# Expert outputs weighted on their way out of PSUM and added by the scatter to the residual rows in DRAM

## The chip, the cores and the metric

The kernel runs on one core of a Trainium2 chip. A core has TensorE (PE; its weight loads are PEld), VectorE (DVE), ScalarE (ACT), GpSimd (POOL), SyncE (SP, which issues most transfers) and 16 DMA engines between DRAM and the core's memory. The metric is the device time of one execution in microseconds (us), as the median of several runs.

## What is computed

A first block (window attention, a gated linear recurrence and a delta-rule recurrence) is followed by two layers on 16 + 1024 tokens of width 1024. Layer 0 has a short convolution as its mixer, layer 1 latent attention. Each ends in a mixture of experts with a residual, which is what the change is about:

```
h = h + mixer(rmsnorm(h, g))
h = h + hier_moe(rmsnorm(h, g2), ...)

hier_moe(x):                       # 64 experts in 8 groups, inner width 256
    grp  = argmax(x @ w_grp);  p_g = max(softmax(x @ w_grp))
    top2 = two largest of softmax(x @ w_exp) inside group grp
    gate = p_g * top_p / sum(top_p)                # two weights per token
    for each expert e:  y_e = (silu(x @ w_gate[e]) * (x @ w_up[e])) @ w_down[e]
    result[token] = sum over its two experts of gate * y_e[token]
```

After layer 0 the rows go, normed, into the latents of the attention (`w_dq`, `w_dkv`); after layer 1 a last norm gives the output, for tokens 16 to 1039.

## The kernel before, in words

Everything is fp32. `moe` runs in two blocks. `back_and_route` (not changed) makes the mixer's output rows, adds the residual and stores the sum in DRAM (`h1` in layer 0, `h3` in layer 1), stores the normed rows in `hn`, and works out for each token its two experts and its rank in each expert's list. From these it makes `queue`: for each pair of experts 128 slots, 64 per expert, row 0 with the token, row 1 with 2 x token + choice; a slot that is not used has a number out of bounds, and the transfer leaves it out. What does not fit into 64 slots of an expert goes to a "spill" loop behind the main one, which is entered only if there is such a rest.

`experts` then goes over 32 pairs of experts. The weights of a pair are 6 MB (`gate`, `up`, `down`, 2 MB each) in a ring of `RING` = 3 slots; SP issues a load as soon as the products that read the slot's old weights are done (`g_done`, `h_done`, `y_done`). For pair p:

- POOL gathers 128 rows of `hn` into `xe` two pairs ahead, as soon as PE has turned pair p (`x_turned`), and then scatters the rows of pair p-2 into `ys` (`scatter`, line 3433). `ys` has one row of 1024 for each token and each of its two choices.
- PE turns the rows (8 transposes), ACT and DVE copy them out (`rows_out`), PE makes the gate and up products (line 3249), ACT the silu, DVE `hidden`, PE turns that, ACT copies it (`hT_copy`), and PE makes the down products (line 3269) of pair p between the gate and up products of pair p+1.
- ACT and DVE copy the two halves of the result out of PSUM (`y_first`, `y_second`, called in `y_half`) into one of two buffers `ysb`; each copy waits until the scatter of two pairs ago has landed (`y_stored`).

The two gate weights per token are made by ACT (two exponentials, line 3560) and DVE (`gates`) at pair 1. The plan of the spill (`spill_plan`, DVE) stands at pair 2.

The results in `ys` are weighted and summed in the stage that follows. `combine_and_latents` (layer 0, line 3713) loads, per tile of 128 tokens, the residual rows from `h1` (0.5 MB) and the `ys` rows (1 MB) in a ring of three buffers; `make` (DVE) adds the two weighted rows with `gathered_sum` (two instructions), POOL stores the sum as `h2`, which the second layer's output stage reads again, and ACT and DVE norm the rows for PE's transposes and latent products. `combine_out` (line 4028) does the same at the end of the kernel for 8 tiles, 5 of them with sums on DVE and 3 on PE, and then norms and stores them. Residual rows of the last stage are issued behind the last weights, in `FinalLoads.start`; `ys` rows when the last scatter has landed, in `rows` (SP waits for `y_stored`). Between the blocks every engine meets in a barrier.

Of the kernel before, what the change touches and what calls it, by code (L numbers as in the profile page):

```python
# [11 lines left out]
P = 128  # L12
# [3158 lines left out]
def experts(nc, D, layer, tokens, keep, spill, gate, gu_slots, d_slots, xe, g_loaded, u_loaded, d_loaded, x_loaded, after, within):  # L3171
# [5 lines left out]
    with Phase(nc, "ex", within) as ph:  # L3177
# [18 lines left out]
        owner = ph.sb("owner", [1, SPILL_BLOCKS, EXPERTS])  # L3196
# [7 lines left out]
        sp_none = ph.sb("sp_none", [P, SPILL_PAIRS])  # L3204
        x_ps = ph.ps("x_ps", [P, 2, 512])
# [10 lines left out]
                                                       "y_stored", "w_used", "x_used", "seen"]}  # L3216
        y_stored = [ph.sem(f"y{b}_stored") for b in range(2)]
        d_ends = [ph.sem(f"d_end{k}_loaded") for k in range(2)]
        hn_dram, y_rows = D["hn"], D["ys"].rearrange("t (c d) -> (t c) d", c=2)
# [12 lines left out]
        def spill_scatter(pool, b, s, pair):  # L3232
            pool.sem_inc(s["out_ready"], 1)
            nc.gpsimd.tensor_copy(ib[:, b, 1:2], queue[:, 1, bass.ds(pair, 1)]).then_inc(s["out_ready"], 1)
            pool.wait_ge(s["out_ready"], 2)
            nc.gpsimd.indirect_dma_start(y_rows[:, :], bass.IndirectOffsetOnAxis(ap=ib[:, b, 1:2], axis=0), ysb[:, b], None,
                                         bounds_check=2 * T - 1, oob_is_err=False).then_inc(s["y_stored"], 16)
            pool.sem_clear(s["out_ready"])
# [72 lines left out]

        def spill_plan(dve, v):
# [3 lines left out]
            dve.wait_ge(id_done, 2)  # L3316
# [8 lines left out]
            v(tt(owner[:], send[0:1].unsqueeze(1).to_broadcast([1, SPILL_BLOCKS, EXPERTS]),  # L3325
                 blocks[0:1].unsqueeze(2).to_broadcast([1, SPILL_BLOCKS, EXPERTS]), ALU.is_le))
            v(red(owners[:, 0:SPILL_BLOCKS], owner[:], AX.X, ALU.add))
# [7 lines left out]
        def spill_slots(dve, v):  # L3335
# [14 lines left out]
            for n in range(2 * TT):  # L3350
                t, c, b = n // 2, n % 2, n % 2
                if n >= 2:
                    dve.wait_ge(hot_used, n - 1)
                v.hold(ts(hot_r[:, b], row[:], rest[:, t, c:c + 1], ids[:, t, c:c + 1], ALU.is_equal, ALU.mult))
                v(ts(hot_b[:, b], blocks[:], at_blk[:, t, c:c + 1], None, ALU.is_equal))
                dve.sem_inc(hot_made, 1)
            dve.wait_ge(hot_used, 2 * TT)
            found = h_ps[:, 1, 0:SPILL_PAIRS]
# [6 lines left out]
        def spill_products(pe):  # L3365

            for n in range(2 * TT):
                pe.wait_ge(hot_made, n + 1)
                for half in range(2):
                    rows = slice(CAP * half, CAP * half + CAP)  # L3370
                    last = nc.tensor.matmul(h_ps[rows, 1, 0:SPILL_PAIRS], hot_r[:, n % 2], hot_b[:, n % 2, half::2],
                                            start=(n == 0), stop=(n == 2 * TT - 1))
                last.then_inc(hot_used, 1)
# [7 lines left out]
        with nc.Block() as block:  # L3381
# [43 lines left out]
            def _(pool):  # L3425
# [30 lines left out]
                with pool.If(0 < count):  # L3456
                    pool.sem_inc(s["seen"], 1)
                    pool.wait_ge(spill_queue, 1)
                    with pool.Fori(0, SPILL_PAIRS) as i:
                        with pool.If(2 * i < count):  # L3460
# [3 lines left out]
                            spill_scatter(pool, 0, s, PAIRS_M + i)  # L3464
                            pool.wait_ge(s["y_stored"], 16 * i + 16)
# [4 lines left out]
            def _(pe):  # L3470
# [15 lines left out]
                for p in range(PAIRS_M):  # L3486
# [47 lines left out]
            def _(act):  # L3534
# [5 lines left out]
                def y_half(p):  # L3540
                    if p >= 2:
                        act.wait_ge(y_stored[p % 2], 16 * (p // 2))
                    act.wait_ge(m["y_done"], p + 1)
                    y_first(p % 2).then_inc(m["y_out"], 1)

                rows_out(0)
                for p in range(PAIRS_M):
# [11 lines left out]
                    if p == 1:  # L3559
                        nc.scalar.activation(gdiff[:], gdiff[:], ACT.Exp).then_inc(gate_exp, 1)  # L3560
                        nc.scalar.activation(ed[:], ed[:], ACT.Exp).then_inc(gate_exp, 1)
# [3 lines left out]
                with act.If(0 < count):  # L3565
                    with act.Fori(0, SPILL_PAIRS) as i:
                        with act.If(2 * i < count):
# [8 lines left out]
                            y_first(0).then_inc(s["y_out"], 1)  # L3576
# [3 lines left out]
            def _(dve):  # L3580
# [6 lines left out]
                def y_half(p):  # L3587
# [3 lines left out]
                    y_second(p % 2).then_inc(m["y_out"], 1)  # L3591

                rows_out(0)
                for p in range(PAIRS_M):
# [7 lines left out]
                    if p == 1:  # L3602
                        gates(dve, v)
# [6 lines left out]
                with dve.If(0 < count):  # L3610
                    spill_slots(dve, Chain(dve, slots_own))
                    with dve.Fori(0, SPILL_PAIRS) as i:
                        with dve.If(2 * i < count):
# [7 lines left out]
                            y_second(0).then_inc(s["y_out"], 1)  # L3621
                after.scale_second(nc, dve)


def gathered_sum(nc, v, y, gate, h, out, t):

    v(nc.vector.scalar_tensor_tensor(out=out, in0=y[:, 0:DM], scalar=gate[:, t, 0:1], in1=h, op0=ALU.mult, op1=ALU.add))  # L3627
    v(nc.vector.scalar_tensor_tensor(out=out, in0=y[:, DM:], scalar=gate[:, t, 1:2], in1=out, op0=ALU.mult, op1=ALU.add))  # L3628


class LatentLoads:


    NBUF = 3

    def __init__(self, nc, ph, D, part, h_in):
        self.D, self.h_in = D, h_in
        self.hb = part(0, self.NBUF, DM)
        self.yb = part(9, self.NBUF, 2 * DM)
        self.y_loaded = [ph.sem(f"latent_y{b}_loaded") for b in range(self.NBUF)]  # L3640
# [8 lines left out]
        self.h_loaded = [ph.sem(f"latent_h{b}_loaded") for b in range(self.NBUF)]  # L3649

    def start(self, sp):
# [4 lines left out]
        self.residual_in(sp, 0)  # L3656
# [4 lines left out]
    def rows(self, sp):  # L3661
        for t in range(self.NBUF):
            self.rows_in(sp, t)
            if t + 1 < self.NBUF:
                self.residual_in(sp, t + 1)

    def residual_in(self, sp, t):
        b = t % self.NBUF
        sp.dma_start(self.hb[:, b], self.h_in[P * t:P * t + P]).then_inc(self.h_loaded[b], 16)
# [14 lines left out]

    def rows_in(self, sp, t):
        b, r = t % self.NBUF, rows_of(t)
        sp.dma_start(self.yb[0:r, b], self.D["ys"][P * t:P * t + r]).then_inc(self.y_loaded[b], 16)
# [25 lines left out]
def combine_and_latents(nc, D, gate, h_in, h_out, part, pre, cq, ckv, kr, next_loads):  # L3713

    QT, CT, KW = QR // P, KVR // P, KVR + ROPE
    with Phase(nc, "cl") as ph:
        NBUF, NOUT = 3, 4
        hb, wq, wk, gains, gq, gk = pre.hb, pre.wq, pre.wk, pre.gains, pre.gq, pre.gk
        yb, y_loaded = pre.yb, pre.y_loaded
        ho = part(15, NOUT, DM)  # L3720
# [25 lines left out]
        (tab_loaded, const_done, made, squared,  # L3746
         rooted, scaled, turned, xT_out, q_done, k_done, lat_sq, lat_rooted, q_out, k_out, lat_turned, lat_out,
         v_own) = (ph.sem(n) for n in (
             "tab_loaded", "const_done", "made", "squared", "rooted", "scaled", "turned", "xT_out", "q_done", "k_done", "lat_sq",
             "lat_rooted", "q_out", "k_out", "lat_turned", "lat_out", "v_own"))  # L3750
        stored = [ph.sem(f"h{n}_stored") for n in range(NOUT)]
        with nc.Block() as block:

            @block.sync
            def _(sp):
                for dst, name in ((cos, "cos_tok"), (sin, "sin_tok")):
                    sp.dma_start(dst[:], D[name]).then_inc(tab_loaded, 16)
                for t in range(NBUF, TT):
                    b = t % NBUF

# [595 lines left out]
```

## Time and profile before

| | us |
|---|---|
| runs, median (lowest to highest) | 2762.22 (2761.85 to 2762.86) |
| span of the profiled execution | 2760.1 |
| PE busy | 2466.4 (89%) |
| DVE busy | 1066.0 (39%) |
| ACT busy | 541.8 (20%) |
| POOL busy | 342.3 (12%) |
| DRAM read, written | 529.06 MB, 65.01 MB |

Of the profiled execution the profile gives only the span; its own time is not shown, and the median of the runs lies 2.1 us above the span. The page cuts the span into 40 slices of 69 us; each digit is a busy share in tenths. In the rows below PE's queue, PE's matmuls and its weight loads are apart. A wait is put down to what ended it. "To landing" is the time from the issue of a transfer until its semaphore is up.

### The profile page before, as it was taken

The numbers are of one execution on the slowest core, as the hardware profiler recorded it, in microseconds if no ns is written. First come the engines' busy times: TensorE is split into PE (matmuls) and PEld (weight loads), VectorE is DVE, ScalarE is ACT, GpSimd is POOL, SyncE is SP. The second block draws the span as 40 slices with busy tenths as digits, with TensorE's granted clock in tenths as the row PEclk, the third lists the DMA queues.
The fourth block names the chain that finished last, engine by engine and source line by source line (L and its number), as shares of the span: only waits on it lengthen the run. The fifth ranks groups of instructions, "written<-read, shape, count | busy, mean of one in ns | idle before, by whom it ended". The sixth has DMA issues, their size and how long they took to land. (4 is left out here: it accounts for less than half of the span.)

```text
span 2760.1 us, 39501 instructions
## 1 busy us (share of the span) xinstructions
PE 2466.4 (89%) x16330; PEld 1535.8 (56%) x16330; DVE 1066.0 (39%) x2180; ACT 541.8 (20%) x1226; POOL 342.3 (12%) x365
## 2 busy tenths in 40 slices
PE   9999988898999998987777899999999989777776
PEld 5444567547888655554444455766674555444443
DVE  3473654666555653211111154445545431111113
ACT  1312455210000011111111141322331111111112
POOL 3321002400000211111111100000003111111110
PEclk9999999999999999999999999999999999999998
DMA  3111010230113136999999970000113499999998
GB/s 118 35 38 53 5 48 5 79 114 34 43 46 119 71 135 246 420 424 425 425 425 426 405 304 24 17 25 8 52 45 137 159 401 425 425 425 426 425 424 341
DMA packets 88726, 566.06 MB, mean 205 GB/s; under 512 B 19408, under 2 KB 19568, under 8 KB 59344
## 3 DMA queue, kind: packets, MB, share of 16 engines
q1 hardware_dynamic: 63504, 506.86, 45.1%
q0 software_dynamic: 20144, 38.79, 3.7%
q10 hardware_dynamic: 4896, 17.83, 1.6%
q8 instruction: 133, 2.18, 0.3%
q14 instruction: 49, 0.40, 0.0%
HBM read 529.06 MB, written 65.01 MB: 215 GB/s over the span
## 5 line engine op out<-in xcount | busy, mean ns | idle before, releaser
L3249 PE MATMUL ex__h_ps<-all__arena,ex__xT 128*64 128x256 f32 x3392 | 406.8, 395 | 108.1 <-DMA all__arena<-in_w_up_t 84.0
L3249 PEld LDWEIGHTS ex__h_ps<-all__arena,ex__xT 128*64 128x64 f32 x3392 | 249.7, 142 | 277.2 <-DMA all__arena<-in_w_up_t 123.3
L3300 DVE COPY ex__ysb<-ex__y_ps 128x512 f32<-128x512 f32 x64 | 44.3, 692 | 493.0 <-PE ex__y_ps L3269 483.0
L3269 PE MATMUL ex__y_ps<-b__w,ex__hT 128*64 128x512 f32 x640 | 146.8, 600 | 27.7 <-issue 27.7
L3429 POOL DMA_INDIRECT b__rows<-s_hn,mo__queue x60 | 60.6, 1010 | 746.0 <-PE ex__x_ps L3242 746.0
L3291 DVE TENSOR_TENSOR ex__hs<-ex__sg,ex__h_ps 128x256 f32<-128x256 f32 x64 | 27.0, 421 | 305.4 <-PE ex__h_ps L3249 305.4
L2534 PE MATMUL cm__acc<-all__arena,cw__w 128*128 128x260 f32 x576 | 136.0, 386 | 2.6 <-PEq L84 2.3
L2534 PE MATMUL cm__acc<-all__arena,cm__sums 128*128 128x260 f32 x576 | 134.3, 383 | 0.0
L2534 PEld LDWEIGHTS cm__acc<-all__arena,cw__w 128*128 128x128 f32 x576 | 110.4, 192 | 20.4 <-issue 3.3
L2534 PEld LDWEIGHTS cm__acc<-all__arena,cm__sums 128*128 128x128 f32 x576 | 109.5, 190 | 17.2 <-issue 0.3
L3282 ACT COPY ex__xT<-ex__x_ps 128x512 f32<-128x512 f32 x64 | 37.4, 585 | 381.0 <-PE ex__x_ps L3242 381.0
L3269 PEld LDWEIGHTS ex__y_ps<-b__w,ex__hT 128*64 128x64 f32 x640 | 48.8, 138 | 105.3 <-issue 102.8
L2920 PE MATMUL hd__o<-all__arena 128*128 128x128 f32 x704 | 96.4, 282 | 6.4 <-ACT all__arena L2990 6.4
L2920 PEld LDWEIGHTS hd__o<-all__arena 128*128 128x128 f32 x704 | 85.0, 191 | 21.5 <-ACT all__arena L2990 14.9
L3249 PE MATMUL ex__h_ps<-mo__wx,ex__xT 128*64 128x256 f32 x704 | 80.8, 382 | 15.0 <-DMA mo__wx<-in_w_gate_t 8.9
L1955 POOL MEMSET mo__ident<- 128x128 f32 x2 | 0.4, 204 | 735.5 <-POOLq L84 735.5
L2075 PE MATMUL pb__acc<-b__w,all__arena 128*128 128x512 f32 x192 | 87.9, 603 | 1.8 <-PEq L84 1.8
L3297 ACT COPY ex__ysb<-ex__y_ps 128x512 f32<-128x512 f32 x64 | 37.5, 586 | 258.1 <-PE ex__y_ps L3269 250.4
L374 PE MATMUL fr__acc<-X__xT,fr__w 128*128 128x512 f32 x192 | 85.3, 594 | 0.0
L3242 PE MATMUL ex__x_ps<-mo__ident,b__rows 128*128 128x128 f32 x512 | 75.7, 292 | 8.6 <-PEq L84 8.6
L3242 PEld LDWEIGHTS ex__x_ps<-mo__ident,b__rows 128*128 128x128 f32 x512 | 63.2, 195 | 34.0 <-issue 34.0
L3434 POOL DMA_INDIRECT s_ys<-ex__ysb,mo__queue x64 | 64.3, 1005 | 110.0 <-DVE ex__ysb L3300 92.9
(550 smaller groups left out, 4111.2 us busy)
## 6 DMA issues: line engine op xcount, KB each, us to landing
all__arena<-in_w_up_t SPq DMA_DIRECT2D x62, 2048.0 KB, 44.1
all__arena<-in_w_gate_t SPq DMA_DIRECT2D x40, 2048.0 KB, 43.2
b__w<-in_w_down_t SPq DMA_DIRECT2D x40, 2048.0 KB, 44.6
mo__wx<-in_w_gate_t SPq DMA_DIRECT2D x22, 2048.0 KB, 44.0
all__arena<-in_w_down_t SPq DMA_DIRECT2D x22, 1024.0 KB, 38.8
mo__wx<-in_w_down_t SPq DMA_DIRECT2D x20, 1024.0 KB, 44.2
all__arena<-s_ys SPq DMA_DIRECT2D x15, 1024.0 KB, 11.3
cw__w<-in_conv_w_in_t SPq DMA_DIRECT2D x24, 512.0 KB, 4.5
```

What stands on the lines that cost most here:

```text
L374: last = mm(acc[:, bank], weight[:, k], moving(k), start=(first and k == 0), stop=(k == HKT - 1), skip_group_check=not first)
L2075: last = mm(acc[:, bank], weight[:, k], moving[:, k], start=(first and k == 0), stop=(last_here and k == HK - 1), skip_group_check=not first)
L2534: last = nc.tensor.matmul(bank(u, x), weight(k), moving(k, c), start=(k == 0), stop=(k == HK - 1))
L2920: last = mm(o_ps[:, h, 0:P], vv[:, s, h], pT[:, h, 4 * g + a], start=(g == 0 and a == 0), stop=(g == end and a == len(tiles_of(i)[g]) - 1))
L3242: last = nc.tensor.transpose(x_ps[:, k // 4, P * (k % 4):P * (k % 4) + P], xe[:, b, k::KT], ident[:])
L3249: last = nc.tensor.matmul(h_ps[half, c, DE * b:DE * b + DE], xT[:, b, k, half], slots[c][:, n, k], start=(k == 0), stop=(k == KT - 1))
L3269: last = nc.tensor.matmul(y_ps[half, c], hT[:, b, k, half], rows[k][:, n, 512 * c:512 * c + 512], start=(k == 0), stop=(k == 1))
L3282: return nc.scalar.copy(xT[:, b, 0:4].rearrange("p k q -> p (k q)"), x_ps[:, 0])
L3297: return nc.scalar.copy(ysb[:, b, 0:512], y_ps[:, 0])
L3300: return nc.vector.tensor_copy(ysb[:, b, 512:], y_ps[:, 1])
L3429: g.indirect_dma_start(xe[:, p % 2], None, hn_dram[:, :], bass.IndirectOffsetOnAxis(ap=queue[:, 0, p:p + 1], axis=0), bounds_check=T - 1, ...
L3434: g.indirect_dma_start(y_rows[:, :], bass.IndirectOffsetOnAxis(ap=queue[:, 1, p:p + 1], axis=0), ysb[:, p % 2], None, bounds_check=2 * T - ...
```

## The change

- The main scatter and the spill scatter write with `compute_op=ALU.add` into the residual rows (`h1` in layer 0, `h3` in layer 1) by token, instead of plainly into `ys`. `ys` and `h2` are gone; the second layer reads `h1`.
- As two experts of one token may be in neighbouring transfers, each scatter first waits until the one before has landed. In the spill loop the two halves of a block go one after the other.
- The copies out of PSUM multiply each slot's row by its weight. For this `gates` moves ahead of pair 0, and a table `slot_gate` (128 slots x 32 pairs) is made with 2 products per token tile and choice on PE (`gates_by_slot`) out of one-hot rows of DVE (`gates_by_rank`). The spill has a table of its own.
- The latents and the last stage load one row per token, after the last scatter has landed, and have no sums; the last stage has no work on PE. `owner` in `spill_plan` is made in two halves.

```diff
@@ experts
+        hn_dram, rows_dram = D["hn"], after.h_in
-        def y_first(b):
-            return nc.scalar.copy(ysb[:, b, 0:512], y_ps[:, 0])
+        def y_first(b, weight):
+            return nc.scalar.activation(ysb[:, b, 0:512], y_ps[:, 0], ACT.Copy, scale=weight)
-        def y_second(b):
-            return nc.vector.tensor_copy(ysb[:, b, 512:], y_ps[:, 1])
+        def y_second(b, weight):
+            return nc.vector.tensor_scalar(ysb[:, b, 512:], y_ps[:, 1], weight, None, ALU.mult)
+        def gates_by_rank(dve, v):
+            for n in range(2 * TT):
+                t, c = n // 2, n % 2
+                if n >= NHOT:
+                    dve.wait_ge(gates_placed, n - NHOT + 1)
+                v.hold(nc.vector.tensor_scalar(by_rank[:, n % NHOT], row[:], rk[:, t, c:c + 1], gate[:, t, c:c + 1],
+                                               ALU.is_equal, ALU.mult))
+                v.wait()
+                dve.sem_inc(weighed, 1)
+        def gates_by_slot(pe):
+            for n in range(2 * TT):
+                t, c = n // 2, n % 2
+                pe.wait_ge(weighed, n + 1)
+                for half in range(2):
+                    slots = slice(CAP * half, CAP * half + CAP)
+                    last = nc.tensor.matmul(y_ps[slots, 1, 0:PAIRS_M], by_rank[:, n % NHOT],
+                                            chosen[:, t, c, PAIRS_M * half:PAIRS_M * half + PAIRS_M],
+                                            start=(n == 0), stop=(n == 2 * TT - 1))
+                last.then_inc(gates_placed, 1)
@@ experts, POOL
                 def scatter(p):
-                    g.indirect_dma_start(y_rows[:, :], bass.IndirectOffsetOnAxis(ap=queue[:, 1, p:p + 1], axis=0),
-                                         ysb[:, p % 2], None, bounds_check=2 * T - 1,
-                                         oob_is_err=False).then_inc(y_stored[p % 2], 16)
+                    if p >= 1:
+                        pool.wait_ge(y_stored[(p - 1) % 2], 16 * ((p - 1) // 2 + 1))
+                    g.indirect_dma_start(rows_dram[:, :], bass.IndirectOffsetOnAxis(ap=queue[:, 0, p:p + 1], axis=0),
+                                         ysb[:, p % 2], None, bounds_check=tokens - 1,
+                                         oob_is_err=False, compute_op=ALU.add).then_inc(y_stored[p % 2], 16)
@@ experts, PE
                 def last_product(p):
+                    pe.wait_ge(gates_out, 1)
...
                     if p + 1 < PAIRS_M:
                         turn(p + 1)
+                    if p == 0:
+                        gates_by_slot(pe)
@@ experts, ACT
+                nc.scalar.activation(gdiff[:], gdiff[:], ACT.Exp).then_inc(gate_exp, 1)
+                nc.scalar.activation(ed[:], ed[:], ACT.Exp).then_inc(gate_exp, 1)
                 rows_out(0)
@@ experts, DVE
                 rows_out(0)
+                gates(dve, v)
+                gates_by_rank(dve, v)
                 for p in range(PAIRS_M):
...
-                    if p == 1:
-                        gates(dve, v)
+                    if p == 0:
+                        dve.wait_ge(gates_placed, 2 * TT)
+                        nc.vector.tensor_copy(slot_gate[:], y_ps[:, 1, 0:PAIRS_M]).then_inc(gates_out, 1)
+                        dve.wait_ge(gates_out, 1)
@@ LatentLoads and FinalLoads
     def rows(self, sp):
-        for t in range(self.NBUF):
-            self.rows_in(sp, t)
...
+        for t in range(self.TT):
+            sp.dma_start(self.hb[:, t], self.h_in[P * t:P * t + P]).then_inc(self.h_loaded[t], 16)
@@ combine_and_latents -> latents
-                    act.wait_ge(made, t + 1)
+                    act.wait_ge(h_loaded[t], 16)
...
-                make(0)
                 scale(0)
-                make(1)
                 scale(1)
@@ combine_out -> normed_out
+            @block.scalar
+                for t in range(TT):
+                    act.wait_ge(h_loaded[t], 16)
+                    nc.scalar.activation(sq[:], hb[:, t], ACT.Square, accum_out=ss[:, t:t + 1]).then_inc(squared, 1)
+                    act.wait_ge(squared, t + 1)
+                    nc.scalar.activation(rt[:, t:t + 1], ss[:, t:t + 1], ACT.Sqrt, scale=1.0 / DM,
+                                         bias=eps[:]).then_inc(rooted, 1)
+            @block.vector
+                for t in range(TT):
+                    dve.wait_ge(rooted, t + 1)
+                    v(nc.vector.reciprocal(rs[:, t:t + 1], rt[:, t:t + 1]))
+                    nc.vector.scalar_tensor_tensor(out=hb[:, t], in0=hb[:, t], scalar=rs[:, t:t + 1], in1=gb[:],
+                                                   op0=ALU.mult, op1=ALU.mult).then_inc(scaled, 1)
```

## Rows read from the trace of the kernel before

**Rows 1.** The page, 40 equal slices: DMA busy tenths and rate.

```profile
DMA  3111010230113136999999970000113499999998
GB/s 118 35 38 53 5 48 5 79 114 34 43 46 119 71 135 246 420 424 425 425 425 426 405 304 24 17 25 8 52 45 137 159 401 425 425 425 426 425 424 341
```

**Rows 2.** Windows: start:end, length, busy PE, PEld, DVE, ACT, POOL, clock, DMA share, GB/s.

```profile
1230.00:1570.00 340.00, 264.58 (x1868) 150.53 (x1870) 37.90 (x63) 38.01 (x83) 40.30 (x40) 0.97 1.01 425
2390.00:2700.00 310.00, 241.36 (x1708) 137.87 (x1704) 34.60 (x58) 35.09 (x77) 36.33 (x37) 0.98 1.01 425
1600.00:1705.00 105.00, 95.83 (x422) 64.19 (x421) 54.23 (x137) 35.33 (x92) 5.29 (x11) 0.98 0.46 178
```

**Rows 3.** Waits of PE, 1230 to 1570 us: total us, times, longest.

```profile
PE ex__h_ps L3249 <- DMA all__arena<-in_w_up_t: 39.7, 20, 2.8
```

**Rows 4.** DMA view, 1230 to 1570 us: queues (packets, MB, share), issues (median landing).

```profile
q1 hardware_dynamic: 10203, 133.04, 92.1%
q0 software_dynamic: 5938, 11.29, 8.7%
...
s_ys<-ex__ysb,mo__queue POOLq DMA_INDIRECT x21, 14.7
b__rows<-s_hn,mo__queue POOLq DMA_INDIRECT x19, 10.6
```

**Rows 5.** Timeline of POOL in layer 0: start, us, line, [idle before].

```profile
1124.86 1.03 POOL L3434 DMA_INDIRECT s_ys<-ex__ysb,mo__queue  x1 [0.30 <-issue]
...
1137.34 1.02 POOL L3434 DMA_INDIRECT s_ys<-ex__ysb,mo__queue  x1 [0.30 <-issue]
...
1306.90 1.00 POOL L3434 DMA_INDIRECT s_ys<-ex__ysb,mo__queue  x1 [0.30 <-issue]
...
1323.17 1.01 POOL L3434 DMA_INDIRECT s_ys<-ex__ysb,mo__queue  x1 [0.30 <-issue]
...
1573.22 0.97 POOL L3434 DMA_INDIRECT s_ys<-ex__ysb,mo__queue  x1 [8.19 <-DVE ex__ysb L3300]
```

**Rows 6.** Around pair 0 of layer 0: timeline, and one line (min/median/max ns).

```profile
L2392 DVE TENSOR_SCALAR pb__hot<-mo__row,mo__rk,mo__ids x34: 304/307/315, 970.7 to 2215.2; 128x64 f32<-128x64 f32 x34
...
1086.60 0.91 PE L2176 MATMUL pb__rk_ps<-mo__chosen,pb__hot 128*64 128x32 f32 x16 [0.60 <-DVEq L2395]
...
1109.20 1.16 PE L3242 MATMUL ex__x_ps<-mo__ident,b__rows 128*128 128x128 f32 x8
...
1109.40 0.42 DVE L3291 TENSOR_TENSOR ex__hs<-ex__sg,ex__h_ps 128x256 f32<-128x256 f32 x1 [8.96 <-PE ex__h_ps L3249]
...
1111.15 3.67 PE L3249 MATMUL ex__h_ps<-mo__wx,ex__xT 128*64 128x256 f32 x32 [0.55 <-DVE ex__xT L3285]
```

**Rows 7.** Timeline of the end of the kernel.

```profile
2716.04 0.98 POOL L3434 DMA_INDIRECT s_ys<-ex__ysb,mo__queue  x1 [13.93 <-DVE ex__ysb L3300]
...
2722.62 1.99 SPq L4025 DMA_DIRECT2D all__arena<-s_ys  x4
...
2726.19 0.20 POOL L1390 MEMSET co__ident<- 128x128 f32 x1 [9.17 <-POOLq L84]
...
2728.79 1.28 ACT L4093 ACT_TABLE_LOAD   x1
...
2751.13 1.06 ACT L4102 ACTIVATE co__sq<-co__ho 128x1024 bf16<-128x1024 f32 x1 [3.15 <-DVE co__ho L4122]
...
2752.53 1.02 ACT L4102 ACTIVATE co__sq<-co__acc 128x1024 bf16<-128x1024 f32 x1
...
2754.23 1.28 DVE L4122 SCALAR_TENSOR_TENSOR co__ho<-co__acc,co__rs,all__arena 128x1024 f32<-128x1024 f32 x1
```

**Rows 8.** Timeline of the end of layer 0's experts and the start of the latents.

```profile
1588.02 0.97 POOL L3434 DMA_INDIRECT s_ys<-ex__ysb,mo__queue  x1 [13.83 <-DVE ex__ysb L3300]
...
1592.04 0.33 SPq L3687 DMA_DIRECT2D all__arena<-s_ys  x1
...
1602.69 1.09 PE L3787 MATMUL cl__tp<-cl__ident,all__arena 128*128 128x128 f32 x8 [2.02 <-DVE all__arena L3939]
```

More of the change, by code:

```diff
@@ L3230, in spill_gather, with spill_scatter, spill_gate_in @@
             pool.sem_clear(s["in_ready"])
[L3232 to L3238, printed above, removed]
+        def spill_scatter(pool, b, s, pair, at):
+            for half in range(2):
+                pool.sem_inc(s["out_ready"], 1)
+                nc.gpsimd.tensor_tensor(ib[:, b, 1:2], queue[:, 0, bass.ds(pair, 1)], half_off[:, half:half + 1], ALU.add
+                                        ).then_inc(s["out_ready"], 1)
+                pool.wait_ge(s["out_ready"], 2)
+                nc.gpsimd.indirect_dma_start(rows_dram[:, :], bass.IndirectOffsetOnAxis(ap=ib[:, b, 1:2], axis=0), ysb[:, b],
+                                             None, bounds_check=tokens - 1, oob_is_err=False, compute_op=ALU.add
+                                             ).then_inc(s["y_stored"], 16)
+                pool.sem_clear(s["out_ready"])
+                pool.wait_ge(s["y_stored"], 32 * at + 16 * half + 16)
+        def spill_gate_in(pool, at):
+            nc.gpsimd.tensor_copy(gate_now[:], spill_gate[:, at]).then_inc(s["g_ready"], 1)
+            pool.wait_ge(s["g_ready"], 1)
+            pool.sem_clear(s["g_ready"])
         def turn_rows(b):
@@ L3324, in spill_plan @@
             v(tt(begin[:], send[:], nspill[:], ALU.subtract))
-            v(tt(owner[:], send[0:1].unsqueeze(1).to_broadcast([1, SPILL_BLOCKS, EXPERTS]),
-                 blocks[0:1].unsqueeze(2).to_broadcast([1, SPILL_BLOCKS, EXPERTS]), ALU.is_le))
-            v(red(owners[:, 0:SPILL_BLOCKS], owner[:], AX.X, ALU.add))
+            for at in range(0, SPILL_BLOCKS, SPILL_BLOCKS // 2):
+                some = slice(at, at + SPILL_BLOCKS // 2)
+                v(tt(owner[:], send[0:1].unsqueeze(1).to_broadcast([1, SPILL_BLOCKS // 2, EXPERTS]),
+                     blocks[0:1, some].unsqueeze(2).to_broadcast([1, SPILL_BLOCKS // 2, EXPERTS]), ALU.is_le))
+                v(red(owners[:, some], owner[:], AX.X, ALU.add))
             v(ts(owners[:, 0:SPILL_BLOCKS], owners[:, 0:SPILL_BLOCKS], float(EXPERTS - 1), None, ALU.min))
@@ L3354, in spill_slots @@
                 v.hold(ts(hot_r[:, b], row[:], rest[:, t, c:c + 1], ids[:, t, c:c + 1], ALU.is_equal, ALU.mult))
+                v.hold(ts(hot_g[:, b], row[:], rest[:, t, c:c + 1], gate[:, t, c:c + 1], ALU.is_equal, ALU.mult))
                 v(ts(hot_b[:, b], blocks[:], at_blk[:, t, c:c + 1], None, ALU.is_equal))
@@ L3370, in spill_products @@
                     rows = slice(CAP * half, CAP * half + CAP)
-                    last = nc.tensor.matmul(h_ps[rows, 1, 0:SPILL_PAIRS], hot_r[:, n % 2], hot_b[:, n % 2, half::2],
-                                            start=(n == 0), stop=(n == 2 * TT - 1))
+                    for bank, hot in ((0, hot_g), (1, hot_r)):
+                        last = nc.tensor.matmul(h_ps[rows, bank, 0:SPILL_PAIRS], hot[:, n % 2], hot_b[:, n % 2, half::2],
+                                                start=(n == 0), stop=(n == 2 * TT - 1))
                 last.then_inc(hot_used, 1)
@@ L3620, in _ @@
                             dve.wait_ge(s["y_done"], i + 1)
[L3621 removed]
+                            y_second(0, gate_now[:]).then_inc(s["y_out"], 1)
                 after.scale_second(nc, dve)
[L3625 to L3628 removed]
 class LatentLoads:
[L3634 removed]
     def __init__(self, nc, ph, D, part, h_in):
         self.D, self.h_in = D, h_in
[L3638 to L3640 removed]
+        self.TT = -(-T // P)
+        self.hb = part(9, self.TT, DM)
         self.wq = part(3, KT, QR)
@@ L3648, in __init__ @@
         self.q_scaled, self.k_scaled = ph.sem("q_scaled"), ph.sem("k_scaled")
-        self.h_loaded = [ph.sem(f"latent_h{b}_loaded") for b in range(self.NBUF)]
+        self.h_loaded = [ph.sem(f"latent_h{t}_loaded") for t in range(self.TT)]
     def start(self, sp):
@@ L3757, in _ @@
                     sp.dma_start(dst[:], D[name]).then_inc(tab_loaded, 16)
-                for t in range(NBUF, TT):
-                    b = t % NBUF
-                    sp.wait_ge(made, t - NBUF + 1)
-                    pre.residual_in(sp, t)
-                    pre.rows_in(sp, t)
                 next_loads(sp)
@@ L3994 @@
     TT = SEQ // P
-    NBUF = 4
     def __init__(self, nc, ph, D, part, h_in):
@@ L4000, in __init__ @@
         self.gb = part(8, DM)
-        self.yb = part(9, self.NBUF, 2 * DM)
-        self.y_loaded = [ph.sem(f"final_y{b}_loaded") for b in range(self.NBUF)]
         self.g_loaded = ph.sem("final_g_loaded")
@@ L4268, in program_parts @@
                 head_w = HeadLoads(nc, lt, D)
-                combine_and_latents(nc, D, gate, D["h1"], D["h2"], part, latent, cq, ckv, kr, head_w.start)
+                latents(nc, D, part, latent, cq, ckv, kr, head_w.start)
                 heads(nc, D, head_w, arena, cq, ckv, kr, oT, out1.start)
             moe(nc, D, 1, SEQ, oT, out1, D["h3"], gate, part, final)
-            combine_out(nc, D, gate, D["h3"], part, final)
+            normed_out(nc, D, final)
 def program(nc, D):
```

190 lines of the change are left out of this document (50 added, 140 removed).

## The prediction

> **What bounds the kernel now.** I read the page's slices first: the DMA engines are full (9) in two stretches, 1100 to 1570 us and 2225 to 2705 us, where they move 425 GB/s, and nearly idle elsewhere [rows 1]. Those are the two expert stages. Then the windows: in the middle of each stage the DMA share is 1.01 at 425 GB/s while PE is busy 265 of 340 us and 241 of 310 us; between the stages, in the latents, it is the reverse, PE 96 of 105 us at a DMA share of 0.46 [rows 2]. Then the waits: PE's longest wait inside the experts is for the up weights, 39.7 us over 20 waits [rows 3]. So each expert stage lasts as long as its bytes take, any byte added there is paid in full, and any engine work added there is paid only if it starves the DMA queue. The DMA view of the same 340 us gives the prices: the weights' queue moved 133.04 MB in 92.1% of the engines' time, POOL's queue (gathers and scatters) 11.29 MB in 8.7%; a scatter lands 14.7 us after issue, a gather 10.6 [rows 4]. POOL's timeline gives the rhythm: scatters are 12.5 us apart while PE catches up with weights already there, 16.3 us once the stream sets the pace, and no scatter waits for another [rows 5]. At the end the last scatter lands, eight 1 MB tiles of `ys` are read, and sums, norm and stores run behind them.
>
> **1. The scatter becomes a read, an add and a write.** Each expert's output row is now added to the residual row in DRAM. The write of 4 KB per row was there before; what is new is that the old row has to be fetched. Layer 0 scatters 1040 tokens x 2 = 2080 rows = 8.52 MB, layer 1 2048 rows = 8.39 MB. About 30 of the 32 scatters of a layer are issued while the stream is full (the 31st goes out at 1573.22 [rows 5], the last after the weights), so 8.0 and 7.9 MB are fetched inside the full stretch. No row of before shows an accumulating transfer. Lower bound: the fetch costs nothing. Upper bound: two more moves of the row (a fetch and a trip of its own for the sum). The nearest row is POOL's queue itself, which is made of just such 4 KB rows: 8.7% of 340 us for 11.29 MB is 29.6 us, 2.62 us per MB [rows 4]. I take one more move at that price, because the engines' share is used up whatever the direction of the bytes (1.01 at 425 GB/s with gathers, scatters and weights mixed [rows 2]): 8.0 x 2.62 = 21.0 us and 7.9 x 2.62 = 20.7 us, **+41.7 us**; bounds 0 and +83.
>
> The Trainium skill, page "Collectives: The Full Stack", section "Part 3: Why 7× under link rate — side-by-side accounting", says the adder in the DMA path is free but a reduce reads two sources through one read ring, so its rate is half that of a copy. By that rule the fetch is exactly one more move, and the sum stays as above; by the row alone (425 GB/s, direction unseen) it could be anything from none to two. No run here shows it yet. It speaks against the change and excludes neither bound.
>
> **2. Each scatter waits for the one before.** POOL waits for `y_stored` of p-1 before it issues scatter p. Behind it on POOL are the gather of p+3 and the next scatter; behind its landing are both `y_half` copies two pairs on, and through them PE. In the steady part the gap between scatters is 16.3 us and a landing takes 14.7 [rows 4, 5], so the wait is already over when POOL comes to it, by 1.6 us; the pair itself grows by 41.7/60 = 0.7 us. If the scatter lands up to 2.3 us later than now, nothing waits. Early on the gap is only 12.5 us, so there POOL does wait; but there the stream is the bound too (slices of 9 from 1100 us on [rows 1]) and PE is ahead of it, so I take 0. When POOL waits, the scatter also moves away from the gather issued 1.3 us before it, in whose shadow it lands now (14.7 against 10.6), which shortens its landing. Bounds: 0, and the rival below.
>
> **3. Gates moved to the front of pair 0.** ACT's two exponentials and their table load run while ACT is idle for the first rows. DVE adds `gates` and 18 (16 in layer 1) products of 307 ns [rows 6], 5.5 us, behind `rows_out(0)`; `hidden(0)` starts at 1109.40 now, some 9 us after `rows_out(0)`, so the first 16 fit, and the last two wait for PE. PE adds 36 (32) products after `turn(1)`; 16 of that shape take 0.91 us [rows 6], so 36 take 2.0 us. They stand before `turn_hidden(0)`, so the gate products of pair 1 start 2 us later than 1111.15, and with them the release of the weight slot. By then SP has issued both loads of pair 3, which wait only for pair 0's products (4 MB, some 10 us at 425 GB/s), and every transfer issued later lands 45 us after issue in the steady part; I take 0. Bounds: 0 and the whole 2 us per layer, +4; were each product its full latency (0.22 us, 8 us in all) perhaps +5 per layer. The old place at p = 1 gives back nothing, for DVE was waiting there. Weighting in ACT's and DVE's copies out of PSUM is one instruction for one. The second half of `owner` and the extra spill matmuls are on engines that wait; the spill loop isn't entered (64 scatters, 32 per layer, is the number of the main loop). 0.
>
> **4. End of layer 0 and latents.** Gone: 8.5 MB of `ys` reads, 4.3 MB of stores of `h2`, two 1.28 us DVE sums per tile. All that lay beside PE, which is busy 96 of 105 us [rows 2], so only the start can gain. Now: last scatter 1588.02, SP issues rows from 1592.04, the first transposes start at 1602.69 [rows 8]. After: nine row loads instead of five take SP some 2 us more before the phase opens (0.5 us each, four in 1.99 [rows 7]); table load and first root take as now, but the wait for the first 1 MB of `ys` and its sum of two 1.28 us instructions go. I take **-0.5 us**, bounds -2 and +2. The accumulating scatter's landing at 4.0 us (1588.02 to 1592.04) gets longer by an estimated fetch latency: **+1.0 us**, bounds 0 and +4.
>
> **5. The last stage.** Now: last scatter issued 2716.04, landed by 2722.62, norm phase at work from 2726.2, end 2760.1 [rows 7]: 44.1 us. After: no residual rows stand in the queue behind the weights any more, so the last landing is nearer layer 0's 4.0 than its own 6.6; with the fetch 5.0, at 2721.0. Eight row issues of 0.5 us, 2725.0; the phase opens 1.5 us later as now, 2726.5. ACT: constant, table load (1.28 us) and a root, 2728.5. Then per tile Square and root: 2751.13 to 2752.53 is 1.40 us [rows 7]; eight are 11.2 us, 2739.7. DVE, with one instruction of 1.28 us and a reciprocal per tile [rows 7], keeps up and ends 1.5 us behind, 2741.2; the last store takes what it takes now, 2760.1 - 2755.5 = 4.6 us, so 2745.8. Reads and stores are 8.4 MB, at 425 GB/s 19.7 us from 2723 on, 2743, so the queue does not bind. I allow 0.7 us for stores between loads: 2746.5, **-13.6 us**, bounds -17 and -8 (were each tile held by loads and stores alternating). The DMA work for `ys` (8.4 MB) is what goes; of the 4.2 MB of residual rows, formerly hidden behind the weights, the load is now exposed, and that is in this sum.
>
> **Sum** against the profiled execution: 2760.1 + 41.7 - 0.5 + 1.0 - 13.6 = 2788.7. The median of the runs, 2762.22, is 2.1 us above that span; so **2790.8 us**.
>
> **Rivals.**
> *A. The fetch is free* (the read side has room that the 425 GB/s don't show, or the row comes back beside the weights). For it: every transfer in [rows 4] either fills or empties the core's memory, none shows a fetch that stays in the DMA path. Against: a share of 1.01 leaves no engine time. Time: 2790.8 - 41.7 = 2749.1, faster. Half free gives 2770.0.
> *B. The chain of scatters becomes the clock.* Place: POOL's wait for `y_stored` of p-1. It decides once a landing under load takes more than the pair's 16.3 + 0.7 = 17.0 us. The scatter's own part of its landing is 14.7 - (10.6 - 1.3) = 5.4 us [rows 4, 5]; if the fetch doubles that, 20.1 us, and if the gap then becomes 20.1, 30 gaps are 603 us against 1573.22 - 1124.86 = 448.4 us now [rows 5], +154.6 us per layer: 2762.2 + 309.2 - 13.1 = 3058. For it: the landing is already 90% of the gap. Against: with the wait the scatter leaves the gather's shadow, and a slower pair empties the queue, both of which shorten the landing. The skill's page "DMA: Bandwidth & Descriptors", section "Queues, rings and completion order", has each engine take turns between queues packet by packet, which would make every fetched row a further turn behind a weight packet; by that the landing is the 20.1 of this rival, not the 15.4 that bytes alone give.
> *C. Two more moves per row, or a slow adder*: +83.4 instead of +41.7, 2832.5, slower. Nothing in the profile excludes it.
>
> **How the numbers follow.** Forecast 0.60 (its own range 2776 to 2805, from the bounds of parts 3 to 5 and 2.35 to 2.9 us per MB). A, whole or in good part, 0.17. B 0.10. C 0.13. The range takes in A nearly whole, the forecast and C's middle: 2749 to 2833, leaving out B, some of C and the edge of A. This kernel's measurement tells 0.2%, 5.5 us, from no change. Faster holds A without its half-free end, 0.17; same 0.05; slower the rest, 0.78.
>
> **What would show it.** Windows inside the experts: DMA share still 1.01 but the weights' rate lower, pairs 0.7 us longer, POOL's queue with about half more engine time (part 1); if the pair time is unchanged, A. Scatter landings of 15 to 17 us, POOL's waits for scatters short and only before 1230 us (2); if scatters stand at equal gaps of their own landing while the DMA share falls below 1.0, B. Start of PE's second pair 2 us later and no dip of the share (3). Last scatter's issue to the end some 30 us instead of 44.1 (5). The forecast is wrong if the distance between the last scatter of each layer and that layer's first grows by less than 10 or more than 30 us.

## The result, and the profile after

The changed kernel takes **2801.96 us** (median of 4 runs, 2801.07 to 2804.15) where the kernel before takes 2762.03 (4 runs, 2761.08 to 2762.86): a ratio of 1.0148, 95% interval 1.0133 to 1.0162. That is 39.9 us slower; forecast were 2790.8 us, +28.6. The profiled execution after has a span of 2799.4 us (time 2801.17), 39.3 more than the 2760.1 before.

The page of the kernel after, DMA busy tenths and rate in 40 equal slices:

```profile
DMA  3111010220112237999999930000103499999997
GB/s 116 38 37 54 1 48 5 100 105 31 46 46 102 101 125 310 406 408 411 411 410 410 360 129 8 17 24 8 57 39 139 171 389 409 410 410 407 411 412 261
```

The engines are as full as before in both expert stages (9), but the rate that the trace shows is 410 and not 425 GB/s [rows 1]. The windows of the kernel after (columns as in [rows 2]) say the same: a share of 1.01 in both expert stages.

```profile
1240.00:1590.00 350.00, 265.49 (x1850) 152.37 (x1848) 39.11 (x63) 40.14 (x83) 52.64 (x40) 0.96 1.01 410
2400.00:2740.00 340.00, 254.31 (x1800) 147.59 (x1796) 37.26 (x60) 38.62 (x80) 51.73 (x39) 0.97 1.01 409
1620.00:1725.00 105.00, 99.14 (x421) 66.01 (x422) 30.24 (x106) 34.85 (x88) 0.55 (x3) 0.95 0.20 79
```

The DMA view of the first of them (queues: packets, MB, share of 16 engines; then issues, the last number the median landing in us), and in the same stretch PE's wait for the up weights (total us, times, longest):

```profile
q1 hardware_dynamic: 10239, 132.07, 88.8%
q0 software_dynamic: 5770, 11.01, 12.4%
...
s_h<-ex__ysb,mo__queue POOLq DMA_INDIRECT x21, 15.3
b__rows<-s_hn,mo__queue POOLq DMA_INDIRECT x19, 10.6
```

```profile
PE ex__h_ps L3266 <- DMA all__arena<-in_w_up_t: 45.1, 21, 3.1
```

Here the fetch can be read, though no row is called by it. POOL's queue moved 11.01 MB, about as much as in [rows 4], but its packets took 12.4% of 350 us, 43.4 us: 3.94 us per MB where [rows 4] give 2.62. At 2.62 the 11.01 MB would take 28.8 us; the other 14.6 us belong to the fetch of the 5.5 MB that the scatters add (half of the queue's bytes), **2.65 us per MB**: one move, at the price of a move. The trace counts its engine time and not its bytes, which is why the rate falls to 410 at a full share. PE waits for weights more than in [rows 3]: it is not what got slower.

Where the 39.3 us went, by the same four marks in both traces (the start of the span, the last scatter of each layer, POOL's first IOTA of layer 1's experts, the end of the span):

```
                                        before     after     difference   forecast
start to layer 0's last scatter        1588.02   1611.98       +24.0       +21.0
last scatter to layer 1's experts       638.86    644.41        +5.5        +0.5
layer 1's experts to its last scatter   489.16    511.45       +22.3       +20.7
last scatter to the end                  44.1      31.6        -12.5       -13.6
```

The end of layer 0 after, POOL, SP and PE (timeline: start, us, engine, line, what, [idle before <- what ended it]); it answers to [rows 8]:

```profile
1598.60 1.54 POOL L3480 DMA_INDIRECT s_h<-ex__ysb,mo__queue  x1 [11.36 <-DMA s_h<-ex__ysb,mo__queue]
...
1611.98 1.56 POOL L3480 DMA_INDIRECT s_h<-ex__ysb,mo__queue  x1 [11.84 <-issue]
1617.52 4.46 SPq L3715 DMA_DIRECT2D all__arena<-s_h  x9
...
1624.00 7.17 PE L3876 MATMUL cl__aq<-all__arena 128*128 128x384 f32 x12 [8.65 <-POOL cl__eps L3801]
...
1631.01 1.04 PE L3814 MATMUL cl__tp<-cl__ident,all__arena 128*128 128x128 f32 x8
```

And the end of the kernel, which answers to [rows 7]:

```profile
2767.84 1.55 POOL L3480 DMA_INDIRECT s_h<-ex__ysb,mo__queue  x1 [12.05 <-DVE ex__ysb L3317]
2773.73 3.77 SPq L4019 DMA_DIRECT2D all__arena<-s_h  x8
...
2778.72 1.28 ACT L4054 ACT_TABLE_LOAD   x1 [11.72 <-PEq L84]
...
2791.64 1.28 DVE L4069 SCALAR_TENSOR_TENSOR all__arena<-all__arena,co__rs 128x1024 f32<-128x1024 f32 x1
```

### The profile page after: what moved, and what is told of

Read it like the earlier page. It is cut to its first block and busy times, and to the rows that moved or that the text cites. A ratio compares the mean times of both kernels' runs of the same rounds, so it can differ in the third digit from the quotient of the medians.

```text
span 2799.4 us, 39801 instructions
## 1 busy us (share of the span) xinstructions
PE 2464.2 (88%) x16430; PEld 1539.5 (55%) x16430; DVE 1043.4 (37%) x2192; ACT 545.9 (19%) x1220; POOL 379.1 (14%) x362
## 5 line engine op out<-in xcount | busy, mean ns | idle before, releaser
L3317 DVE TENSOR_SCALAR ex__ysb<-ex__y_ps,ex__slot_gate 128x512 f32<-128x512 f32 x64 | 48.0, 750 | 526.9 <-PE ex__y_ps L3286 508.8
L3480 POOL DMA_INDIRECT s_h<-ex__ysb,mo__queue x64 | 102.6, 1604 | 205.8 <-DMA s_h<-ex__ysb,mo__queue 141.2
L3314 ACT ACTIVATE ex__ysb<-ex__y_ps,ex__slot_gate 128x512 f32<-128x512 f32 x64 | 44.0, 687 | 270.0 <-PE ex__y_ps L3286 258.5
```

What stands on the lines that cost most here:

```text
L3314: return nc.scalar.activation(ysb[:, b, 0:512], y_ps[:, 0], ACT.Copy, scale=weight)
L3317: return nc.vector.tensor_scalar(ysb[:, b, 512:], y_ps[:, 1], weight, None, ALU.mult)
L3480: g.indirect_dma_start(rows_dram[:, :], bass.IndirectOffsetOnAxis(ap=queue[:, 0, p:p + 1], axis=0), ysb[:, p % 2], None, bounds_check=toke ...
```

## The experiments

Every kernel is compared with the kernel before on the same chip. That took 2759.03 us (16 runs, 2755.87 to 2768.4) beside four of them (the addition taken out, the wait alone, the fetch apart, 28 fillers), and 2760.67 (7 runs, 2759.64 to 2766.2) beside the other three (each scatter twice, 16 fillers, half the width). Theory F is the prediction's part 1: the stream is full, and the fetch is one more move of each row. Its rivals are the prediction's A, B and C, and that the weighting or the moved gates cost the time.

**The addition taken out** of the main loop's scatter, all else as changed.

```diff
-  oob_is_err=False, compute_op=ALU.add).then_inc(y_stored[p % 2], 16)
+  oob_is_err=False).then_inc(y_stored[p % 2], 16)
```

> The changed kernel with the main scatter writing plainly (no add), so the residual and one of a token's two experts are lost from the result; the waits between scatters, the weighting, the table of gates and the short last stage all stay. Theory F (the fetch of the old rows is paid in full in the DMA stream): the experts are as long as before the change, last up products about 500 us after the first pair as before, scatter issue 1.0 us again, the whole about 22 + 23 + 2 us (chain at the end of layer 0) + 2 us (landings) below the changed kernel's 2802: 2753, that is 9 below before. Rival W (the wait of each scatter for the one before it is what costs): the time stays within 5 us of 2802. Rival G (weighting and gates cost): likewise about 2800.

Measured: 2751.12 us (7 runs, 2742.66 to 2758.07), 0.9964 [0.9946, 0.9982] of the kernel before, 1.9 us below the 2753 expected and 50.8 us below the changed kernel's 2801.96 (by the two ratios, 1.0148 and 0.9964, it is the same). The rate is back, and POOL's queue is back at its old price (window, then queue, 1240 to 1550 us):

```profile
1240.00:1550.00 310.00, 240.21 (x1716) 136.36 (x1714) 35.43 (x57) 36.66 (x76) 38.32 (x38) 0.98 1.01 425
```

```profile
q1 hardware_dynamic: 9187, 121.14, 92.0%
q0 software_dynamic: 5479, 10.43, 8.8%
```

8.8% of 310 us for 10.43 MB is 2.62 us per MB. The expert stages of this kernel, first IOTA to last scatter, last 489.5 and 490.3 us, before 490.3 and 489.2. So the weighted copies, the waits, the moved gates and the memsets together cost the experts nothing; everything they lost is in the one argument of this diff.

**The wait alone**, added to the kernel before.

```diff
+  if p >= 1:
+      pool.wait_ge(y_stored[(p - 1) % 2], 16 * ((p - 1) // 2 + 1))
```

> The kernel before, with one thing added: scatter p waits on POOL until scatter p-1 has landed. Theory F: 2762, within 3 us, as a landing of 14.7 us fits into the pair's 16.3 us and the early pairs have slack. The end of a layer may show the wait: last-but-one scatter issued 14.8 us before the last, landing 14 to 15 us, at most +1 us per layer. Rival W: +35 to +40 us, 2800.

Measured: 2759.11 us (10 runs, 2756.6 to 2761.56), 0.9999 [0.9989, 1.0008]. POOL's waits of this kernel, 1090 to 1240 us and then 1240 to 1550 us, show that it does wait; the time shows that nothing comes later for it:

```profile
POOL s_ys L3436 <- DMA s_ys<-ex__ysb,mo__queue: 28.3, 8, 5.2
```

```profile
POOL s_ys L3436 <- DMA s_ys<-ex__ysb,mo__queue: 7.5, 4, 2.8
```

**The fetch as a transfer of its own.** No addition, but from pair 3 on an ordinary gather of the same rows behind each scatter, into a tile that nobody reads (29 of 32 pairs in each layer).

```diff
-  oob_is_err=False, compute_op=ALU.add).then_inc(y_stored[p % 2], 16)
+  oob_is_err=False).then_inc(y_stored[p % 2], 16)
+  if p >= 3:
+      ...
+      g.indirect_dma_start(over[...], None, hn_dram[:, :],
+                           bass.IndirectOffsetOnAxis(ap=queue[:, 0, p:p + 1], axis=0), ...).then_inc(fetched, 16)
```

> As e1 (plain write, so the sums are lost from the result), and behind each scatter from p = 3 on POOL gathers the same 128 slots' rows of the normed input into a buffer nobody reads: 29 of 32 fetches per layer, as ordinary transfers without an add. Theory F (what is paid is one more 4 KB move per row): 29/30 of e1's saving is given back in the stream, about +20 us per layer over e1, some 2795; DMA share stays 1.01 and the visible rate goes back up to 425 GB/s, as this fetch is counted. Rival A2 (the adder itself is slow, a plain fetch would cost less): clearly below 2785. Rival O (an extra transfer costs more than its bytes by its turns in the queue): above 2810.

Measured: 2799.7 us (4 runs, 2797.68 to 2801.72), 1.015 [1.0133, 1.0167], where the changed kernel has 1.0148 [1.0133, 1.0162]. The same window and queues:

```profile
1240.00:1550.00 310.00, 242.89 (x1632) 136.56 (x1629) 33.58 (x55) 34.74 (x72) 55.51 (x55) 0.93 1.01 424
```

```profile
q1 hardware_dynamic: 8828, 116.00, 88.1%
q0 software_dynamic: 8059, 15.13, 12.8%
```

The weights get 88.1% here and 88.8% after; POOL's queue takes 12.8% (2.62 us per MB again) and 12.4%. What differs is that this fetch is counted, so the rate reads 424. From layer 0's first IOTA to the start of its last up products it is 501.4 us here (1095.76 to 1597.15), 501.3 after, and 479.0 without any fetch. So the adder itself costs nothing that can be measured. The time is 4.7 us above the 2795 expected, and not all of it is stream: layer 0's last scatter goes out 19.0 us behind the one before it, where the changed kernel has 13.4. By the DMA view the one before had landed after 8.1 us and its own rows were copied at 1606.92, so the last 4.8 us are time for which the profile names no cause. The price agrees with the Trainium skill, "Collectives: The Full Stack", section "Part 3: Why 7× under link rate — side-by-side accounting", which says of the reduce of collectives that the addition is free and the second source halves the rate; here 2.65 us per MB for the second read beside 2.62 for a plain move.

**Each accumulating scatter twice**, the second behind the landing of the first.

```diff
+  for again in range(2):
+      if again:
+          pool.wait_ge(y_stored[p % 2], 16 * (2 * (p // 2) + 1))
       g.indirect_dma_start(rows_dram[:, :], ..., compute_op=ALU.add).then_inc(y_stored[p % 2], 16)
```

> The changed kernel with each accumulating scatter issued twice, each waiting for the one before (the experts' rows are added two times). Theory F (each pass costs its bytes, a write and a fetch, 5.2 us per MB of row): 8 MB more rows per layer, +42 us per layer, +84 in all, about 2884. Rival B (the chain of landings becomes the clock): two landings in a pair, 15.3 + about 9 us and two issues, 26 us where the pair has 17: about 30 x 9 = +270 us per layer, above 3100, POOL waiting for scatters in every pair and the DMA share below 1. A middle (landings shorten as the stream empties, two of 9 to 11 us): pairs of 20 to 22 us, +100 to +150 us per layer, 3000 to 3100; the rival's mechanism all the same.

Measured: 3091.14 us (4 runs, 3087.86 to 3100.98), 1.12 [1.1173, 1.1227]: the middle case. One pair of it in POOL's timeline, and the window and landings of 1240 to 1550 us:

```profile
1397.29 1.55 POOL L3483 DMA_INDIRECT s_h<-ex__ysb,mo__queue  x1 [4.35 <-DMA s_h<-ex__ysb,mo__queue]
1399.15 1.06 POOL L3473 DMA_INDIRECT b__rows<-s_hn,mo__queue  x1 [0.30 <-issue]
1410.65 1.58 POOL L3483 DMA_INDIRECT s_h<-ex__ysb,mo__queue  x1 [10.44 <-DVE ex__ysb L3317]
1420.85 1.56 POOL L3483 DMA_INDIRECT s_h<-ex__ysb,mo__queue  x1 [8.61 <-DMA s_h<-ex__ysb,mo__queue]
```

```profile
1240.00:1550.00 310.00, 212.11 (x1350) 116.44 (x1350) 25.19 (x45) 28.76 (x60) 63.02 (x45) 0.82 0.91 339
```

```profile
s_h<-ex__ysb,mo__queue POOLq DMA_INDIRECT x30, 9.7
```

30 scatters in 310 us are 15 pairs of 20.7 us, two landings of 9.7 and little more. The share is 0.91: the stream is no longer the bound, the chain is. The second scatter and its fetch would cost some 84 us by bytes; they cost 289. Rival B's mechanism is real, and it decides where the landings of a pair outlast the 17.0 us that the stream gives a pair. The scatter at 1410.65 waits for the landing of 1397.29's, and so does the copy that refills that scatter's buffer, which starts at 1409.87; so "<-DVE" stands for the same landing.

**More filler products** behind layer 0's last scatter, 28 and then 16 instead of 8. The theory, called C in these two expectations and not the prediction's rival C: PE's 8.65 us of idle time before the latents cost the granted clock at their start. The windows of the kernel after, before that gap, at the warm-up products, and behind them (columns as in [rows 2]):

```profile
1600.00:1615.00 15.00, 13.95 (x64) 6.08 (x60) 3.56 (x10) 5.21 (x10) 1.71 (x2) 1.00 0.43 122
1624.00:1630.50 6.50, 6.50 (x11) 3.64 (x12) 0.92 (x2) 2.07 (x5) 0.00 (x0) 0.53 1.02 417
1632.00:1645.00 13.00, 11.90 (x46) 7.89 (x46) 2.40 (x8) 7.46 (x17) 0.00 (x0) 1.00 0.63 253
```

The granted clock is 1.00 (2.4 GHz), 0.53 (the lower level, 1.2 GHz, nearly throughout), and 1.00 again.

```diff
-  for n in range(8):
+  for n in range(8 if layer else 28):      # the second kernel: else 16
```

> The changed kernel with 28 in place of 8 filler matmuls behind the last products of layer 0, so that PE has work for some 9 us more while the last scatter lands and the rows are issued. Theory C (PE stood still 8.7 us before the latents, the clock fell, and the 12 warm-up products took 7.2 us where they took 4.1 before): they take 4.1 again, the first transposes come 3 to 4 us earlier, 2798.5. Rival: the rows, not PE, set the start of the latents (time unchanged, 2802), or the filler delays the phase (slower).

> The changed kernel with 16 filler products instead of 8 behind layer 0's last scatter (28 took 24.3 us of PE and ran past the phase's start; 8 took 7.1 us, so 16 should take about 14 us and end near 1622 us, just before the latents open at 1623). Theory C (the gap of 8.65 us in which PE is idle costs the granted clock at the start of the latents, and with it about 3 us: warm-up products 7.17 us against 4.14): PE idle under 3 us again, warm-up products 4.1 us, first transposes at about 1628 instead of 1631.0, total 2.5 to 3.5 us less than the changed kernel. Rival (the latents' later start is SP's nine row issues and the rows' own landing, the clock is beside it): warm-up back at 4.1 us, total unchanged within 1 us.

Measured with 28: 2807.44 us (4 runs, 2804.77 to 2811.65), 1.0173 [1.0156, 1.019], a miss. I had mis-sized the fillers: 28 of them (56 records) keep PE 24.3 us and hold the phase's start back to 1636 us. With 16: 2800.66 us (4 runs, 2795.81 to 2804.96), 1.0147 [1.013, 1.0164], no difference that can be told. PE's timeline with 28, and SP's and PE's with 16:

```profile
1610.05 24.30 PE L3567 MATMUL ex__x_ps<-b__rows,mo__ident 128*128 128x512 f32 x56
1636.23 4.14 PE L3876 MATMUL cl__aq<-all__arena 128*128 128x384 f32 x12 [1.88 <-POOL cl__eps L3801]
```

```profile
1613.33 5.71 SPq L3715 DMA_DIRECT2D all__arena<-s_h  x9
...
1621.95 0.10 POOL L3801 MEMSET cl__eps<- 128x1 f32 x1
...
1622.10 4.14 PE L3876 MATMUL cl__aq<-all__arena 128*128 128x384 f32 x12 [1.88 <-POOL cl__eps L3801]
...
1626.08 1.04 PE L3814 MATMUL cl__tp<-cl__ident,all__arena 128*128 128x128 f32 x8
```

The clock's part is as the theory had it: with PE idle only 1.88 us, the twelve warm-up products take 4.14 us in both kernels and not 7.17, and from the phase's constants to the first transposes it is 4.1 us (1621.95 to 1626.08) instead of 7.2 (1623.85 to 1631.01). But the total is the rival's: unchanged within 1.3 us, where theory C expected 2.5 to 3.5 less. From the last scatter to the first transposes it is 17.9 us with 16 fillers (1608.13 to 1626.08) and 19.0 with 8, a gain of 1.1 and not of 3. Two things took the other 2 us. SP's nine row issues took 5.71 us against 4.46; that is not the fillers' doing, for they took 5.74 in the kernel without the addition, with 8 fillers, and 4.49 with 28. And the 16 fillers (32 records) keep PE 14.0 us and end at 1620.22, 1.2 us behind SP's last issue (1619.04); the phase's first constant (L3801) stands 2.9 us behind that issue, where it stands 1.9 us behind it with 8 fillers.

**Expert rows at half the width**, in the kernel before.

```diff
-  ysb = ph.sb("ysb", [P, 2, DM])
+  ysb = ph.sb("ysb", [P, 2, DM], mybir.dt.bfloat16)
   ... (also ys in DRAM, its tiles in the latents and the last stage, and spread)
```

> The kernel before, with the expert rows (ysb, the array ys and its tiles in the latents and in the last stage) in bfloat16 instead of fp32: it rounds the experts' rows, and in three tiles of the last stage the gates, to 8 bits of mantissa. Theory F (bytes in the full stretch are paid at 2.6 us per MB, whatever they are for): 4 MB less written per layer inside the stream, -10.5 us per layer, -21; last stage reads 4.2 MB less of ys, -4 to -9 us; total 2730 to 2736. Rival (a price per packet, not per byte: rows of 2 KB cost as much as rows of 4 KB): experts unchanged, only the end shorter, 2750 to 2756.

Measured: 2737.86 us (4 runs, 2733.26 to 2741.86), 0.9915 [0.9896, 0.9933] of the kernel before: the fastest kernel here, at the price of the rounding. It is 1.9 us above the 2730 to 2736 expected. Its expert stages last 479.7 and 479.3 us, 10.5 and 9.9 less than before, as expected, and the end 39.9 instead of 44.1, at the short side of what was expected. Its window and queue:

```profile
1240.00:1550.00 310.00, 244.11 (x1750) 136.51 (x1746) 34.31 (x57) 35.16 (x77) 38.58 (x38) 0.98 1.01 425
```

```profile
q0 software_dynamic: 4336, 8.05, 6.8%
```

6.8% of 310 us for 8.05 MB is 2.62 us per MB with rows of 2 KB too: the price goes by bytes at these sizes. Theory F's account thus holds in both directions, 4 MB fewer as well as 8 MB more.

## Why the prediction was right

The sign, the mechanism and the range held; the time came out 11.2 us above the forecast, 39.9 us of change where 28.6 were forecast, and near the upper end of the forecast's own 2776 to 2805.

1. **The fetch** (forecast +41.7): right. One more move at 2.65 us per MB, not none (rival A) and not two (rival C). By the marks above the stages grew by 24.0 + 22.3 = 46.3 (0.4 of the 24.0 stands before layer 0's experts); against the kernel without the addition, by 24.3 and 21.2. By the prediction's own mark, first to last scatter of a layer, they grew by 21.8 us (463.2 to 485.0) and 21.7 (461.7 to 483.4), well inside its 10 to 30. In layer 0 the stream itself, up to its last up products, ends 21.9 us later (1577.53 to 1599.40), where 21.0 was forecast: the weights' queue moves 51.89 MB instead of 53.92 from 1100 to 1240 us, which is 5 us, and the rest comes behind that, at 0.7 us per pair as forecast: from the 9th to the 27th scatter a pair takes 17.0 us instead of 16.3. The term that was too small is the end, "the last after the weights", costed at nothing: counted from 0, scatter 31 goes out at 1611.98, 2.8 us after its copy had ended (1609.16), where the kernel before takes 0.8 (1587.23 to 1588.02). That is the 2 us on top. It is not the wait for scatter 30: that one, issued at 1598.60, had landed after 10.0 us by the DMA view, at 1608.6. The profile puts the gap down to "issue", that is, to nothing that it shows, and its cause stays open. It comes and goes: in the profiled run with 16 fillers the last scatter left 1.0 us after its copy, and the stage, from first IOTA to last scatter, took 511.7 us instead of 513.8.
2. **The wait** (0): right where the stream sets the pace, as the wait alone shows. One sign did not hold: POOL's waits for scatters were to come only before 1230 us, but from 1240 to 1590 us there are six more, 20.3 us in all, the longest 11.4 near the layer's end; the kernel without the addition waits there too and loses nothing by it. Landings under load stayed at 15.3 us, below the 17.0 from which the prediction let rival B decide. The 20.1 us that it worked out for that rival, with the turn by packets of the Trainium skill's "DMA: Bandwidth & Descriptors", section "Queues, rings and completion order", did not appear: a landing of an accumulating scatter takes 15.3 us where a plain one takes 14.7 [rows 4], or 15.0 with the wait. So the fetch does not double the scatter's part of the landing; the turn by packets itself no run here tests.
3. **The gates** (0): right. PE's 36 short products (72 records) took 2.29 us, and the gate products of pair 1 start at 1113.28 instead of 1111.15 [rows 6], the 2 us forecast, and the stream doesn't notice.
4. **End of layer 0** (+0.5): too low by 5 us, the largest miss of a single step. Landing 5.5 us instead of 4.0 [rows 8] (forecast 5.0; the +1.0 was an estimate that no row gave); from the issue of the rows to the phase's constants 6.3 us instead of 4.4, right at "some 2 us more"; but the warm-up products at the lower clock (7.17 us at 0.53) held the first transposes to 1631.01 although the first row tile was scaled by 1627.1. The forecast had the -2 or so of the dropped sum cancel the issues. In this execution the clock ate it; with the clock given back, the 16 fillers show 1.1 us of gain up to the transposes and the same total, so the clock is a part of this miss and the chain of issues another. A further 1.2 us lie between the transposes and layer 1's experts. Most of the miss does not hang on the addition: without it this stretch is 643.1 us, 4.3 more than before.
5. **The last stage** (-13.6): right within 1.1 us. Landing 5.9 for 5.0, issues 3.8 for 4.0, 1.37 us per tile for 1.40, but 6.5 us from the last DVE instruction to the end for 4.6. Eight 0.5 MB stores now leave within 10 us; that they are the reason is not shown.

The sum against the profiled execution: 3.0 (1, layer 0) + 5.0 (4) + 1.6 (1, layer 1) + 1.1 (5) is 10.7, all by which the span of 2799.4 exceeds the forecast's 2788.7. That it adds up is no check, since the marks divide the whole span. The 1.6 us of layer 1 has no cause shown: even the kernel without the addition differs from the kernel before by -0.7 and +1.1 us in the two stages.

## What to carry over

Where the DMA engines are full, price every edit in bytes moved at the stream's own rate, and count an accumulating write as two moves although the profile's rate and byte counts show one: its cost is in the queue's share of engine time. An addition moved into the transfer pays only if the work that it replaces stood on the path. Here layer 0's sums did not, and only the last stage got shorter, by 12.5 us, for some 8.4 MB of fetches per layer in a full stream. Halving the width of what the stream carries is worth more than moving where it is added. And a chain of scatters that wait for each other costs next to nothing while one landing fits in the time of a pair, and 289 us once two are needed. This kernel chains them because neighbouring ones may add to the same row; no run leaves the wait out beside the addition.

## What the hardware showed that was not expected

- An accumulating indirect scatter of 128 rows keeps POOL 1.55 to 1.6 us at issue, a plain one 1.0 (mean 1604 against 1005 ns, 64 of each). POOL, busy 14% of the span, had the time for it.
- A copy out of PSUM that scales by a column takes longer than a plain one: 750 against 692 ns on DVE and 687 against 586 ns on ACT, 128x512 fp32. The page after:

```profile
L3317 DVE TENSOR_SCALAR ex__ysb<-ex__y_ps,ex__slot_gate 128x512 f32<-128x512 f32 x64 | 48.0, 750 | 526.9 <-PE ex__y_ps L3286 508.8
...
L3480 POOL DMA_INDIRECT s_h<-ex__ysb,mo__queue x64 | 102.6, 1604 | 205.8 <-DMA s_h<-ex__ysb,mo__queue 141.2
```

- The fetch shows outside the stream too: with little or nothing else in the queues, an accumulating scatter had landed 5.5 and 5.9 us after issue when SP took up its rows; the plain one, in the changed kernel without the addition, 3.0 and 2.8.
- 5.4 us of idle time on PE came before a slower start as well. Without the addition the twelve warm-up products took 6.39 us behind 5.37 us of idle time, at a granted clock of 0.63 on average, against 4.14 us at 1.00 behind 1.9 to 3.1 us.
